# Two blocks in one kernel: gates and forgetting queries and keys of the second block projected as one 512-column product

## The reference, cut to what matters

```python
    h = rms_norm_2(x, gain)
    proj = jnp.einsum('bsd,de->bse', h, w_in)
    (qa, ka, va, ga, qb, kb_, vb_, gb, qc, kc, vc, gc,
     q_idx, k_idx, w_idx, f_logit, merge_logit) = jnp.split(proj, SPLIT_POINTS, axis=-1)
    oa = moba_attention(rope_partial(heads(qa, HEADS_A), pos), rope_partial(heads(ka, HEADS_A), pos),
                        heads(va, HEADS_A)).reshape(B, S, WIDTH) * jax.nn.silu(ga)
    ob = dsa_attention(...).reshape(B, S, WIDTH) * jax.nn.silu(gb)
    oc = forgetting_attention(heads(qc, HEADS_C), heads(kc, HEADS_C), heads(vc, HEADS_C),
                              log_f).reshape(B, S, WIDTH) * jax.nn.silu(gc)
    y = jnp.einsum('nbsw,nwd->bsnd', jnp.stack([oa, ob, oc], axis=0), w_branch)
    merged = jnp.sum(gates * y, axis=2)
    return x + jnp.einsum('bsd,de->bse', merged, w_out)
```

## Time and profile before

| | |
|---|---|
| median of 3 runs | 1073.27 us (1071.59 to 1073.71) |
| profiled execution: its time, its span | 1073.57 us, 1071.6 us |
| TensorE busy | 1050.7 us, 98% |
| VectorE busy | 733.7 us, 68% |
| ScalarE busy | 591.6 us, 55% |
| mean granted TensorE clock | 0.995 of 2.4 GHz |

### The profile page before, as it was taken

How to read it: one execution, slowest core, us unless ns; L and a number is a source line. 1 busy time by engine, 2 the same in 40 slices (tenths; PEclk the granted TensorE clock), 3 DMA queues, 4 the chain that set the end, 5 groups by cost and what they waited for, 6 DMA issues and landing times.

```text
span 1071.6 us, 18030 instructions
## 1 busy us (share of the span) xinstructions
PE 1050.7 (98%) x6797; PEld 885.6 (83%) x6797; DVE 733.7 (68%) x1577; ACT 591.6 (55%) x1209; POOL 2.6 (0%) x10
## 2 busy tenths in 40 slices
PE   5999999999999999999999999999999999999997
PEld 3677776788997779989898988889988898888886
DVE  4635567666597756787778766658788778765665
ACT  4534245543265446567766764445567677665444
POOL 0000000000000000000000000000000000000000
PEclk9999999999999999999999999999999999999999
DMA  9997651222342324565555466666464545555662
GB/s 326 337 319 235 182 182 40 60 60 62 97 122 66 80 69 125 147 171 143 137 142 153 144 168 184 191 193 177 131 175 138 139 138 158 156 161 176 195 211 84
DMA packets 203550, 165.41 MB, mean 154 GB/s; under 512 B 7100, under 2 KB 172712, under 8 KB 203464
## 3 DMA queue, kind: packets, MB, share of 16 engines
q1 hardware_dynamic: 202944, 163.28, 52.0%
q0 software_dynamic: 192, 0.66, 0.2%
q10 hardware_dynamic: 328, 0.32, 0.1%
HBM read 163.18 MB, written 1.05 MB: 153 GB/s over the span
## 4 chain that ended last, share of the span: by engine, by line
PE 92%; DVE 4%; ACT 1%; issue 1%; DMA 0%; ACTq 0%; DVEq 0%
PE pj L2072 24%; PE pj L2074 23%; PE pj L2073 23%; PE pj L2166 1%; PE tr L2623 1%; DVE w_lo L1338 1%; PE ac L2427 1%; PE ac L2562 1%; PE sc L2271 1%; PE tr L2278 1%; PE sc L2413 1%; PE ac L2292 1%; PE sc L2544 1%; PE sc L2542 1%; ACT w_hi L835 1%
## 5 line engine op out<-in xcount | busy, mean ns | idle before, releaser
L1338 DVE TENSOR_TENSOR w_lo<-raw,w_hi 128x1024 fp32r<-128x1024 f32 (+2 forms) x258 | 309.4, 1202 | 143.0 <-ACT w_hi L835 141.9
L835 ACT ACTIVATE w_hi<-raw 128x1024 fp32r<-128x1024 f32 (+2 forms) x258 | 268.0, 1040 | 91.0 <-PE pj L2074 87.4
L2072 PE MATMUL pj<-h_hi,w_hi 128*128 128x256 f32 (+1 forms) x960 | 299.6, 312 | 0.2
L2074 PE MATMUL pj<-h_hi,w_lo 128*128 128x256 f32 (+1 forms) x960 | 291.8, 304 | 0.0
L2073 PE MATMUL pj<-h_lo,w_hi 128*128 128x256 f32 (+1 forms) x960 | 291.6, 304 | 0.0
L2072 PEld LDWEIGHTS pj<-h_hi,w_hi 128*128 128x128 f32 x960 | 184.1, 192 | 19.2 <-issue 10.4
L2074 PEld LDWEIGHTS pj<-h_hi,w_lo 128*128 128x128 f32 x960 | 184.2, 192 | 7.5
L2073 PEld LDWEIGHTS pj<-h_lo,w_hi 128*128 128x128 f32 x960 | 184.4, 192 | 6.3
L2072 PE MATMUL pj<-w_hi,h_hi 128*128 128x512 f32 x344 | 137.4, 399 | 2.8 <-DVE w_lo L1338 1.6
L2074 PE MATMUL pj<-w_hi,h_lo 128*128 128x512 f32 x344 | 134.2, 390 | 0.0
L2073 PE MATMUL pj<-w_lo,h_hi 128*128 128x512 f32 x344 | 134.2, 390 | 0.0
(11 more groups left out here) (358 smaller groups left out, 1472.7 us busy)
## 6 DMA issues: line engine op xcount, KB each, us to landing
raw<-in_w_in_dram SPq DMA_DIRECT2D x152, 512.0 KB, 3.8
ada_raw<-in_ada_w_dram SPq DMA_DIRECT2D x48, 512.0 KB, 7.6
raw<-in_even_w_in_dram SPq DMA_DIRECT2D x28, 512.0 KB, 5.2
raw<-in_w_branch_dram SPq DMA_DIRECT2D x24, 512.0 KB, 3.7
raw<-in_w_out_dram SPq DMA_DIRECT2D x16, 512.0 KB, 3.8
raw<-in_odd_w_in_dram SPq DMA_DIRECT2D x11, 512.0 KB, 4.0
raw<-in_even_w_out_dram SPq DMA_DIRECT2D x8, 512.0 KB, 3.7
raw<-in_odd_w_out_dram SPq DMA_DIRECT2D x8, 512.0 KB, 3.8
```

The lines of the kernel that those rows point to most:

```text
L835: last = nc.scalar.activation(hi, src, ACT.Copy)
L1338: last = nc.vector.tensor_tensor(lo, src, hi.bitcast(F32), ALU.subtract)
L2072: nc.tensor.matmul(dst, lh, rh, start=first, stop=False)
L2074: return nc.tensor.matmul(dst, ll, rh, start=False, stop=final)
```

## The change

The high and low part of `h` become two halves of one tensor, `h_both`. For the 12 gate chunks of each layer and the 8 query and key chunks of the forgetting branch, the two matmuls that share the high weight become one of 512 columns, whose left half is the product with the high part of `h` and whose right half the product with the low part. The third matmul (low weight, high `h`) stays at 256 columns and adds to the left half. The bank then holds two halves that must be added: ScalarE copies the left half to SBUF and VectorE adds the right half from the bank. For a gate, the copy goes to `ntmp`, tanh and multiply read the sum there, ScalarE's order becomes copy, `split_hi`, tanh, and VectorE's becomes sum, `split_lo`, the two multiplies (in a pair step: masked scores, sum, `split_lo`, reciprocals, the two multiplies). A bank is freed by VectorE's add.

```diff
+def is_folded(name, i):
+    return name == "g" or (name in ("q", "k") and BRANCH_ORDER[i // 4] == FORGET)
...
-        h_hi, h_lo = sb("h_hi", [P, KT, TOK], F32R), sb("h_lo", [P, KT, TOK], F32R)
+        h_both = sb("h_both", [P, 2, KT, TOK], F32R)
+        h_hi, h_lo = h_both[:, 0], h_both[:, 1]
...
                         elif kind == "g":
                             if i >= 2:
-                                act.wait_ge(*freed_at(G2_OF[("g", i - 2)], lay))
+                                act.wait_ge(og_set, lay * NTRIP + i - 1)
...
-                            nc.scalar.activation(tanh[:, i % 2, 0:SEQ], src, ACT.Tanh, scale=0.5).then_inc(tanh_set, 1)
+                            nc.scalar.activation(tanh[:, i % 2, 0:SEQ], ntmp[:, 2 * (i % 2), :], ACT.Tanh, scale=0.5)\
+                                .then_inc(tanh_set, 1)
...
+                def gate_copy(c):
+                    i = B2_CHUNKS[c][1]
+                    proj_ready(act, G2_OF[("g", i)], lay)
+                    if i >= 2:
+                        act.wait_ge(og_set, lay * NTRIP + i - 1)
+                    nc.scalar.activation(ntmp[:, 2 * (i % 2), :], bank(G2_OF[("g", i)])[:, 0:SEQ], ACT.Copy).then_inc(gate_part, 1)
...
-                    if 1 <= s <= B2_IN:
+                    gate = 1 <= s <= B2_IN and B2_CHUNKS[s - 1][0] == "g"
+                    if gate:
+                        gate_copy(s - 1)
+                    elif 1 <= s <= B2_IN:
                         h_evacuate(s - 1)
...
                     if 1 <= s <= B2_IN:
                         split_hi(pos(s, lay) + AHEAD)
+                    if gate:
+                        h_evacuate(s - 1)
...
+                        if kind in ("q", "k") and is_folded(kind, i):
+                            dve.wait_ge(part_set, lay * len(FOLDED_QK) + FOLDED_QK.index(c) + 1)
...
+                            nc.vector.scalar_tensor_tensor(dst, bank(g)[:, SEQ:TOK], QK_SCALE if kind == "q" else 1.0, dst,
+                                                           ALU.mult, ALU.add).then_inc(freed["dve"], 1)
...
-                            nc.vector.scalar_tensor_tensor(a, tanh[:, i % 2, 0:SEQ], 1.0, bank(g)[:, 0:SEQ], ALU.add,
-                                                           ALU.mult).then_inc(freed["dve"], 1)
-                            dve.wait_ge(*freed_at(g, lay))
+                            after(nc.vector.scalar_tensor_tensor(a, tanh[:, i % 2, 0:SEQ], 1.0, a, ALU.add, ALU.mult))
...
+                def gate_sum(c):
+                    if B2_CHUNKS[c][0] == "g":
+                        i = B2_CHUNKS[c][1]
+                        g, a = G2_OF[("g", i)], ntmp[:, 2 * (i % 2), :]
+                        dve.wait_ge(gate_part, lay * NTRIP + i + 1)
+                        nc.vector.tensor_tensor(a, a, bank(g)[:, SEQ:TOK], ALU.add)\
+                            .then_inc(freed["dve"], 1)
...
                         head_scores(2 * t)
                         head_scores(2 * t + 1)
+                        gate_sum(s - 1)
                         split_lo(pos(s, lay) + AHEAD)
                         head_reciprocal(2 * t)
                         head_reciprocal(2 * t + 1)
-                    if 1 <= s <= B2_IN:
+                    gate = 1 <= s <= B2_IN and B2_CHUNKS[s - 1][0] == "g"
+                    if gate and t is None:
+                        gate_sum(s - 1)
+                    elif 1 <= s <= B2_IN and not gate:
                         h_evacuate(s - 1)
                     if 5 <= s <= B2_IN and t is None:
                         split_lo(pos(s, lay) + AHEAD)
+                    if gate:
+                        h_evacuate(s - 1)
...
+            def products_folded(dst, term, first, final):
+                lh, ll, both = term
+                if final:
+                    nc.tensor.matmul(dst[:, 0:SEQ], ll, both[:, 0, :], start=False, stop=False)
+                    return nc.tensor.matmul(dst, lh, both, start=False, stop=True)
+                nc.tensor.matmul(dst, lh, both, start=first, stop=False)
+                return nc.tensor.matmul(dst[:, 0:SEQ], ll, both[:, 0, :], start=False, stop=False)
...
+                if is_folded(kind, i):
+                    return [(wh[:, k, :], wl[:, k, :], h_both[:, :, k, NORMED[lay]]) for k in range(kt)], TOK
```

More of the change, by code:

```diff
@@ L141, in chunk_groups @@
             "qi": "act", "q": "act", "k": "act", "g": "dve", "out": "dve"}
+    if is_folded(name, i):
+        return [(name, i, "dve")]
     if name == "wkv":
@@ L214 @@
 LAST_GROUP += [GB + lay * NG2 + LAST_OF_CHUNK2.get(c, -1) for lay in range(LAYERS_2) for c in range(C2)]
+FOLDED_QK = [c for c, x in enumerate(B2_CHUNKS) if is_folded(*x) and x[0] != "g"]
 PARTIALS = [c for c, x in enumerate(B2_CHUNKS) if is_partial(*x)]
@@ L579, in build_program @@
         recip_set = sem("recip_set")
+        part_set, gate_part = sem("part_set"), sem("gate_part")
         og_set, g_hi_set, g_lo_set = sem("og_set"), sem("g_hi_set"), sem("g_lo_set")
@@ L1168, in h_evacuate @@
                             continue
-                        proj_ready(act, g, lay)
+                        if kind == "g":
+                            act.wait_ge(*freed_at(g, lay))
+                        else:
+                            proj_ready(act, g, lay)
+                        signal = part_set if is_folded(kind, i) else freed["act"]
                         if kind == "qi":
@@ L1175, in h_evacuate @@
                                 dst = q_h if kind == "q" else k_h
-                                nc.scalar.activation(dst[:, i % NQK, :], src, ACT.Copy, scale=scale).then_inc(freed["act"], 1)
+                                nc.scalar.activation(dst[:, i % NQK, :], src, ACT.Copy, scale=scale).then_inc(signal, 1)
                             else:
-                                h_rope_input(rope_free(i), kind == "k", scale, src)
+                                h_rope_input(rope_free(i), kind == "k", scale, src, signal)
                         elif kind == "v":
@@ L1196, in h_evacuate, with h_rope_input @@
                                 .then_inc(freed["act"], 1)
-                def h_rope_input(n, place, scale, src):
+                def gate_copy(c):
[4 more added lines that the diff above has]
+                    nc.scalar.activation(ntmp[:, 2 * (i % 2), :], bank(G2_OF[("g", i)])[:, 0:SEQ], ACT.Copy).then_inc(gate_part, 1)
+                def h_rope_input(n, place, scale, src, signal):
                     act.wait_ge(rope_out, ROPES1 + lay * ROPES2 + n)
-                    nc.scalar.activation(rope[:, int(place), :], src, ACT.Copy, scale=scale).then_inc(freed["act"], 1)
+                    nc.scalar.activation(rope[:, int(place), :], src, ACT.Copy, scale=scale).then_inc(signal, 1)
                 def h_turned(use):
@@ L1829, in h_evacuate @@
                         g = G2_OF[(kind, i)]
+                        if kind in ("q", "k") and is_folded(kind, i):
+                            dve.wait_ge(part_set, lay * len(FOLDED_QK) + FOLDED_QK.index(c) + 1)
+                            if BRANCH_ORDER[i // 4] == FORGET:
+                                dst = (q_h if kind == "q" else k_h)[:, i % NQK, :]
+                            else:
+                                dst = rope[:, int(kind == "k"), :]
+                            nc.vector.scalar_tensor_tensor(dst, bank(g)[:, SEQ:TOK], QK_SCALE if kind == "q" else 1.0, dst,
+                                                           ALU.mult, ALU.add).then_inc(freed["dve"], 1)
                         if kind == "k" and BRANCH_ORDER[i // 4] != FORGET:
@@ L1833, in h_evacuate @@
                         elif kind == "g":
-                            proj_ready(dve, g, lay)
+                            a, b = ntmp[:, 2 * (i % 2), :], ntmp[:, 2 * (i % 2) + 1, :]
                             dve.wait_ge(tanh_set, 16 + lay * NTRIP + i + 1)
-                            a, b = ntmp[:, 2 * (i % 2), :], ntmp[:, 2 * (i % 2) + 1, :]
-                            nc.vector.scalar_tensor_tensor(a, tanh[:, i % 2, 0:SEQ], 1.0, bank(g)[:, 0:SEQ], ALU.add,
-                                                           ALU.mult).then_inc(freed["dve"], 1)
-                            dve.wait_ge(*freed_at(g, lay))
+                            after(nc.vector.scalar_tensor_tensor(a, tanh[:, i % 2, 0:SEQ], 1.0, a, ALU.add, ALU.mult))
                             dve.wait_ge(o2_set, lay * NTRIP + i + 1)
@@ L2124, in project @@
                             pe.wait_ge(moving[0], moving[1](k))
-                        last = products(bank(g)[:, 0:n], terms[k], n_k == 0, n_k == kt - 1)
+                        form = products_folded if is_folded(kind, i) else products
+                        last = form(bank(g)[:, 0:n], terms[k], n_k == 0, n_k == kt - 1)
                     if k1 == kt:
```

## The result

The changed kernel takes 1078.04 us, median of 4 runs (1077.45 to 1079.46); the kernel before took 1072.43 us on the same chip (4 runs, 1071.13 to 1073.71). The ratio is 1.0053 with a 95% interval of 1.0039 to 1.0066: slower by 5.6 us, where 8.5 had been forecast. The profiled execution has a span of 1077.5 us against 1071.6.

What follows compares the result with a forecast made beforehand. TensorE's stream, busy 98%, sets the end if ScalarE and VectorE deliver in time. With TensorE's savings included, layers ending 4.6 and 3.9 us later make 8.5 on 1073.57, 1082.1, less 0.3 to the median: 1081.8 us; range 1069.0 to 1084.5.

Steps and rivals of the forecast that it cites:

- the walk: Step-by-step lateness through both layers, ending 4.6 and 3.9 us later: 1081.8 us, range 1080 to 1084.5, chance 0.38.
- half of it adds up: Queues recover between steps 29 and 37; TensorE 1 to 3.5 us behind after each layer: 1075.4 to 1080, chance 0.24.
- TensorE's saving: In 40 folded chunks, 0.0124 us saved per k tile, 0.1 us per chunk: 4.0 us in all.
- Step 26 makes the masked scores of step 29 1.1 us late: Gate step 26's work in one row makes chunk 29's split 0.75 late; with k6's add, scores start 546.15 instead of 545.04.
- The prediction's own sign of a wrong size: Wrong by size if ScalarE's waits for gated output in steps 27, 30 and 43 are shorter than 0.5 to 1 us.
- The new chain: In pair steps with a gate, exponentials queue behind sum and tanh; in step 29 this makes the scaling 1.45 us later.
- Step 33: Pair step: chunk 32's split 2.5 late, masked scores 562.3 instead of 559.40, scaling 3.25 late, TensorE 1.3 us behind.
- Chunk 36: Its split_lo follows rotation and scaling, at 569.6 instead of 566.38, 3.2 us late; TensorE 2.3 us behind.
- Steps 37, 41 and 45: Later pair steps: masked scores 3.15, 4.5 and 5.8 us late; TensorE 3.6, 3.8 and 5.1 us behind.
- 0.5 us back behind step 50: At each layer's end, the five gates g7 to g11 give back 5 x 0.1 = 0.5 us.
- The layers, 4.6 and 3.9 us: First layer ends 4.6 us later; second 3.9, with room of 1.45 instead of 0.7 us before what follows step 41.
- The rival on the other side: Nothing slips: lateness ahead of step 37 stays under 0.5 us, TensorE gains all 4.0 us: 1069.3, chance 0.2.

Runs made afterwards that it cites:

- experiment 1: Kernel before with TensorE's part of the fold alone (512-column matmuls in 40 chunks, no copy, no add, order as before): 1069.55 us, ratio 0.9967.
- experiment 2: Kernel before with only query and key chunks folded: 1072.53 us, ratio 0.9992; changed kernel with only gates folded: 1078.01 us, ratio 1.0051.
- experiment 3: Changed kernel with tanh, in pair steps with a gate only, behind both heads' exponentials and ahead of the scaling: 1075.14 us, ratio 1.0012.
- experiment 6: Changed kernel with multiplies ahead of split_lo in other gate steps; in pair steps, sum behind reciprocals and tanh behind scaling: 1077.23 us, ratio 1.0052.
- experiments 4 and 5: Kernel before with only pair-step tanh held for all masked scores: 1073.05 us; with only other gate steps' tanh and multiplies behind the splits: 1073.37 us.
- wait alone: Kernel before with only tanh of pair steps held back until all masked scores are there, no copy, no sum: 1073.05 us, ratio 1.0004.

## Why the prediction was right in direction and too large by 2.9 us

The mechanism and the places were those forecast, and the walk's own range (1080 to 1084.5) was missed. The measured time fell to the rival "half of it adds up" (1075.4 to 1080), by terms that were sized wrongly and not by that rival's mechanism: the queues did not recover between steps 29 and 37, where the masked scores of steps 33 and 37 are 1.31 and 1.32 us late. In the block, where the first block's scatter is out, the change costs 6.4 us and the forecast is too large by 2.1. All lateness in this section is against before without a correction for the start, as in the prediction.

- **TensorE's saving**, 4.0 us: it is 2.8 (experiment 1). In the trace a folded tile takes (508.61 - 506.49) / 6 = 0.353 us in one place and (540.75 - 539.02) / 5 = 0.346 us in another; the forecast 0.347 holds in the second only. I had added the rhythm of rows of one width each; a stream that alternates the two doesn't keep it everywhere.
- **Hidden up to step 26**: right. There was no wait of TensorE, and the exponentials of step 25 followed TensorE's lead (0.67 us early).
- **Step 26 makes the masked scores of step 29 1.1 us late**: this is the step that failed. They came 0.20 early (544.84 against 545.04). The split of chunk 29, forecast 0.75 late, was at 538.84, 0.2 us early. The 0.35 us that VectorE waited before those scores was a wait for TensorE's scores, though its row names a round of the selection: in "TensorE alone" these scores move 0.64 us forward with TensorE. In the row after, no such wait is left. I had laid step 26's work end to end as lateness and had not let the two queues inherit TensorE's head start. The prediction's own sign of a wrong size came in two of its three places: ScalarE's wait for the gated output, to which it gave 0.5 to 1 us in steps 27, 30 and 43, is 0.48, nothing and 1.03.
- **The new chain, 1.45 us**: right in kind, 3.65 - 2.45 = 1.20 us in each pair step with a gate, in both layers.
- **Step 33, scores 2.9 late, TensorE 1.3 behind**: scores 1.31 late (560.71), TensorE 0.79 ahead. The difference of 1.6 is that of step 29's scaling handed on, 1.00 late instead of 2.55.
- **Chunk 36, TensorE 2.3 behind**: 568.99 against 568.47, 0.5 behind, with a wait of 0.78 us for `w_lo` as named.
- **Steps 37, 41 and 45, scores 3.15, 4.5 and 5.8 late, TensorE 3.6, 3.8 and 5.1 behind**: scores 1.32, 2.50 and 3.82 late, TensorE 1.35, 1.70 and 2.65 behind by the first transpose, and by the fourth, which the walk went by, 1.7 (581.19 against 579.48) and 3.0 in steps 38 and 46. From step 30 to 46 TensorE lost 3.7 us where the walk had 4.4, so the growth was sized nearly right and the start wasn't. The stretch took 60.1 us where 61 had been named.
- **0.5 us back behind step 50**: it wasn't given back. In the first layer a wait of 0.3 us for `w_lo` behind gates 8 to 11 took some 0.3 more; in the second, without that wait, 0.2 came back from step 54 on.
- **The layers, 4.6 and 3.9 us**: the first lost 3.9 (it ended 3.38 late after a start 0.50 early), the second 6.4 - 3.9 = 2.5. That the second loses less was argued from the room of 1.45 us in step 42. At step 46, counted from each layer's start, it is 0.9 us less late (2.26 against 3.15), where 0.7 had been forecast; the other 0.5 comes behind step 54 and was not forecast.
- **The rival on the other side** (nothing slips, it decides if the lateness ahead of step 37 stays under 0.5 us): it was 1.3. Queries and keys alone (experiment 2) are a case in which that rival is true.

The experiments add what the walk had only assumed. The loop has two halves, the pair's chain (experiment 3) and the gate's finished output (experiment 6), and each costs next to nothing by itself (experiments 4 and 5) while it takes the other and the 19 us of added work on the two engines to fill the room. What stays open is why a folded tile takes 0.353 us in one chunk and 0.346 in another; that wasn't tried.

## What to carry to other kernels

When an edit gives TensorE a few nanoseconds per matmul and takes instructions of 0.4 us from the engines that feed it, follow one step from each added wait to the next wait of TensorE, and subtract the room found there once, for all additions together: here a wait that cost 0.4 us alone cost 5.1 us on top of the other additions. Start such a walk from the head start that the edit has given by then, and not from the old places. And fold where the result isn't in a loop: the same edit in the query and key chunks alone kept what it saved, 1.2 us.

## What the runs showed of the hardware

The granted clock of TensorE dips for 3.4 us at a time in some executions, with TensorE busy through the dip. In windows of 10 us it shows as 0.83 to 0.98; windows laid inside it give the lower of the two levels (1.2 of 2.4 GHz), 0.50. Windows of the kernel before (PE, PEld, DVE, ACT, POOL busy; clock, DMA share, GB/s):

```profile
440.00:450.00 10.00, 10.00 (x73) 9.84 (x72) 6.63 (x20) 3.89 (x8) 0.00 (x0) 0.83 0.39 104
...
218.10:221.40 3.30, 3.30 (x9) 2.54 (x9) 2.89 (x15) 0.00 (x0) 0.00 (x0) 0.50 0.58 161
440.00:443.30 3.30, 3.30 (x18) 3.30 (x17) 2.92 (x13) 0.00 (x0) 0.00 (x0) 0.50 0.00 0
```

What a dip costs is read from an instruction ahead of it and the same one behind it. VectorE's splits around 440 us, first in the kernel before, then in "wait alone", whose clock is 1.00 there:

```profile
442.19 1.22 DVE L1338 TENSOR_TENSOR w_lo<-raw,w_hi 128x1024 fp32r<-128x1024 f32 x1
445.63 1.22 DVE L1338 TENSOR_TENSOR w_lo<-raw,w_hi 128x1024 fp32r<-128x1024 f32 x1
```

```profile
441.38 1.22 DVE L1342 TENSOR_TENSOR w_lo<-raw,w_hi 128x1024 fp32r<-128x1024 f32 x1
443.33 1.22 DVE L1342 TENSOR_TENSOR w_lo<-raw,w_hi 128x1024 fp32r<-128x1024 f32 x1
```

The distance is 3.44 us against 1.95, so the dip costs 1.5 us; around 218 us the same reading gives 226.84 - 216.35 = 10.49 against 226.03 - 217.12 = 8.91, 1.6 us. Of the eleven traces used here four have a dip near 220 us and one near 440 us, two (the kernel after is one) have one near 23 us and one near 440 us, one has only that near 440 us, and four have none. The four without reach the first pair's transposes 2.1 to 2.5 us earlier than the kernel before: it loses 3.1 us in its two dips and was some 0.8 us ahead of "wait alone" up to then. All these dips lie ahead of the first pair's transposes at 478 us. So this is scatter of the part that no kernel here changes, as large as the effects that were looked for, and the measure that starts behind it is why effects of a few tenths of a microsecond could be read.
